# Moving a store and its reloads to another queue, weights ahead of parameters, three reorderings

## The reference

```python
def first_block(x, ...):                   # one layer
    h = rms_norm(x, norm1_w)
    z = h @ w_in                           # s5 mixer, differential attention, two gates
    m = sigmoid(gs) * (s5_mixer(z) @ w_proj_ssm) + sigmoid(ga) * (diff_attention(z) @ w_proj_attn)
    x = x + m @ w_out
    h = rms_norm(x, norm2_w)
    return x + (silu(h @ w_ffn_gate) * (h @ w_ffn_up)) @ w_ffn_down

def second_block(x, positions, ...):       # two layers
    for l in range(2):
        cb, cc, ch, cg, cq, ckv, kpe, mg, rcols, rg = split(x @ w_in[l])
        y_conv = cb * conv3(cc * ch) * silu(cg)
        q = (rms_norm(cq) @ w_uq)          # per head: 128 plain columns and 64 rotary ones
        kv = (rms_norm(ckv) @ w_ukv)
        y_mla = attention(q with rope(q_pe), k with rope(kpe), v) * silu(mg)
        y_rwkv = rwkv7(rcols) * silu(rg)
        x = layer_norm(4 ** 0.25 * x + concat(y_conv, y_mla, y_rwkv) @ w_out[l]) * ln_g + ln_b
    return x
```

## Time and profile before

| | us |
|---|---|
| median of three runs | 2587.32 |
| lowest, highest | 2584.78, 2589.74 |
| the profiled execution, its own time | 2588.43 |
| its span on the core | 2586.6 |
| mean granted TensorE clock, share of full | 0.985 |
| PE busy | 2484.6 (96% of the span) |
| DVE, ACT, POOL busy | 1475.0, 1130.2, 167.7 |

### The profile page before, as it was taken

How to read it: one execution, slowest core, us unless ns; L and a number is a source line. 1 busy time by engine, 2 the same in 40 slices (tenths; PEclk the granted TensorE clock), 3 DMA queues, 4 the chain that set the end, 5 groups by cost and what they waited for, 6 DMA issues and landing times.

```text
span 2586.6 us, 45207 instructions
## 1 busy us (share of the span) xinstructions
PE 2484.6 (96%) x19625; PEld 2259.6 (87%) x19625; DVE 1475.0 (57%) x1814; ACT 1130.2 (44%) x1562; POOL 167.7 (6%) x172
## 2 busy tenths in 40 slices
PE   6999999999989999999999999999999889999997
PEld 6777888999889999999888899999888789999885
DVE  3899955665445444454444446646555547455555
ACT  4565555544444444444333335324443525334442
POOL 4000000001000000000000002200000231200000
PEclk9999999999999999999999999999999889999998
DMA  7444444455546565655555565434537454235364
GB/s 206 136 155 139 155 142 129 131 188 174 188 140 183 180 185 182 184 183 182 187 186 187 182 202 158 119 88 122 148 127 240 135 181 141 88 102 163 104 198 161
DMA packets 261174, 412.43 MB, mean 159 GB/s; under 512 B 52912, under 2 KB 73776, under 8 KB 260464
## 3 DMA queue, kind: packets, MB, share of 16 engines
q1 hardware_dynamic: 259520, 408.22, 51.4%
q0 software_dynamic: 1424, 1.31, 0.3%
q10 hardware_dynamic: 32, 0.01, 0.0%
HBM read 403.17 MB, written 6.30 MB: 158 GB/s over the span
## 4 chain that ended last, share of the span: by engine, by line
PE 86%; DVE 7%; ACT 2%; SPq 2%; POOL 1%; issue 1%; DMA 1%; ACTq 0%; DVEq 0%
PE bank L569 85%; DVE wp_lo L1077 2%; ACT wp_hi L1727 1%; DMA raw<-w_in 1%; POOL xt L2305 1%; SPq L521 1%; SPq L510 1%; POOL xt L2303 0%; PE bank L776 0%; ACT L1727 0%; DVE r_a L1555 0%; DVE rsd L1202 0%; DVE nsd L1469 0%; DVE r_kb L1557 0%; DVE xr L1720 0%
## 5 line engine op out<-in xcount | busy, mean ns | idle before, releaser
L1077 DVE TENSOR_TENSOR wp_lo<-raw,wp_hi 128x1024 fp32r<-128x1024 f32 x740 | 919.5, 1249 | 950.9 <-ACT wp_hi L1727 949.7
L1727 ACT ACTIVATE wp_hi<-raw 128x1024 fp32r<-128x1024 f32 x740 | 783.4, 1061 | 1180.5 <-PE bank L569 1121.8
L569 PE MATMUL bank<-XX_hi,wp_hi 128*128 128x256 f32 x3840 | 1117.5, 291 | 42.4 <-DVE wp_lo L1077 26.0
L569 PE MATMUL bank<-XX_lo,wp_hi 128*128 128x256 f32 x3840 | 1091.4, 284 | 0.0
L569 PE MATMUL bank<-XX_hi,wp_lo 128*128 128x256 f32 x3840 | 1091.0, 284 | 0.0
L569 PEld LDWEIGHTS bank<-XX_hi,wp_hi 128*128 128x128 f32 x3840 | 741.4, 193 | 62.1 <-issue 37.8
L569 PEld LDWEIGHTS bank<-XX_lo,wp_hi 128*128 128x128 f32 x3840 | 741.9, 193 | 2.2 <-issue 1.9
L569 PEld LDWEIGHTS bank<-XX_hi,wp_lo 128*128 128x128 f32 x3840 | 741.2, 193 | 0.0
L569 PE MATMUL bank<-wp_hi,FF_hi 128*128 128x512 f32 x352 | 139.3, 396 | 0.0
L569 PE MATMUL bank<-wp_lo,FF_hi 128*128 128x512 f32 x352 | 139.1, 395 | 0.0
L569 PE MATMUL bank<-wp_hi,FF_lo 128*128 128x512 f32 x352 | 139.1, 395 | 0.0
(11 more groups left out here) (469 smaller groups left out, 2741.8 us busy)
## 6 DMA issues: line engine op xcount, KB each, us to landing
raw<-w_in SPq DMA_DIRECT2D x304, 512.0 KB, 3.8
raw<-w_out SPq DMA_DIRECT2D x96, 512.0 KB, 4.5
raw<-w_ffn_gate SPq DMA_DIRECT2D x88, 512.0 KB, 3.6
raw<-w_ffn_up SPq DMA_DIRECT2D x88, 512.0 KB, 3.7
raw<-w_ffn_down SPq DMA_DIRECT2D x88, 512.0 KB, 3.6
raw<-w_proj_attn SPq DMA_DIRECT2D x16, 512.0 KB, 4.2
raw<-w_proj_ssm SPq DMA_DIRECT2D x16, 512.0 KB, 3.6
raw<-w_glu SPq DMA_DIRECT2D x8, 512.0 KB, 3.3
```

The costliest lines, as they stand in the source:

```text
L569: return e.matmul(o, lhsT, rhs, start=start, stop=stop, skip_group_check=True)
L1077: return tt(d, src, hi, SUB)
L1727: return e.activation(o, x, func, bias=bias, scale=scale)
```

## The change

1. **The start.** Piece 3 is loaded ahead of the s5 parameters. `ssm_c` is loaded ahead of piece 6, positions and the second constants ahead of piece 8. A semaphore of its own (`s_c5`) covers `ssm_c`. In the first norm, ACT and DVE split each of the first three weight pieces ahead of the group of x instead of behind it.
2. **The norms at `wo3` and `xo3` of layer 0.** DVE evacuates the last job's banks first and splits the piece afterwards. ACT loads the table for the square root one job earlier.
3. **x for the residual.** POOL stores `kept`, for layer 0 once `fd3` is evacuated, for layer 1 behind its own last addition. POOL also reloads the quarters of `xr`, `lng` and `lnb`: the first behind the attention output, each other one when the job before it is over. DVE waits for each quarter by a semaphore of its own.
4. **The rotary part.** `pq` comes ahead of `nq0`. The rotary work on PE, POOL and DVE stands behind `nq0` instead of behind `kn1`, and `MXr_lo` behind `vn1`.

```diff
+        add(f"pq{l}", Wq, [(192 * i + 128, 64) for i in range(8)], 4, "AV")
         for c in range(2):
             add(f"nq{c}{l}", Wq, [(192 * (4 * c + i), 128) for i in range(4)], 4, "AV")
-        add(f"pq{l}", Wq, [(192 * i + 128, 64) for i in range(8)], 4, "AV")
...
-        for p in range(3):
+        for p in range(4):
             weights(p)
...
-        for p in range(3, NP):
-            for l, (name, s, value) in enumerate((("misc0", *freed("fd3", 1)), ("rk1", *YT("b", 7)))):
-                if p == OF[name].over:
-                    e.wait_ge(s, value)
-                    e.dma_start(tokens(kept[l]), xt).then_inc(s_kept, 16)
...
-                        e.dma_start(xr[:, :, w], tokens(kept[l])[:, :, w]).then_inc(s_xr, 16)
...
+        for p in range(4, NP):
+            if p == 6:
+                for d, name in ((X1, "ssm_c_re"), (X2, "ssm_c_im")):
+                    for q in range(2):
+                        e.dma_start(d[:, :, 64 * q:64 * q + 64], cv(name)).then_inc(s_c5, 16)
+            elif p == 8:
+                e.dma_start(posi[:, :], A["positions_2"][0].partition_broadcast(128)).then_inc(s_pos, 16)
+                e.dma_start(cst[:, NFIRST:NCONST], A["consts"][:, NFIRST:NCONST]).then_inc(s_cst, 16)
@@ tensor @@
-            main(at.until(f"kn1{l}"))
+            main(at.until(f"nq0{l}"))
             emptied(e, f"pq{l}")
@@ vector @@
-                e.wait_ge(s_xr, 16 * (4 * l + c + 1))
+                e.wait_ge(s_xr[c], 16 * (l + 1))
...
-                    if p + 3 < NP:
+                    if p + 3 < NP and not (t + 1 == ENDS[j.name] and j.name in ("wo3", "xo30")):
                         split(p + 3)
...
         for g in range(10):
+            if g < 3:
+                split(g)
             if g < 8:
                 rest_of_x(0, g)
-            if g < 3:
-                split(g)
...
         at.limit("fd3")
+        split(OF["wo3"].over + 2)
         roots(1)
...
-            main(at.until(f"kn1{l}"))
-            for i in range(2):
-                e.wait_ge(*RXA("h", 2 * l + i))
-                lo(MXr.lo(512 * i, 512 * i + 512), pair(mixT, 6 + i), ...)
+            main(at.until(f"nq0{l}"))
...
             main(at.until(f"vn1{l}"))
+            for i in range(2):
+                e.wait_ge(*RXA("h", 2 * l + i))
+                lo(MXr.lo(512 * i, 512 * i + 512), pair(mixT, 6 + i), ...)
...
+                    if g == 1:
+                        split(OF["xo30"].over + 2)
@@ scalar @@
+        main(at.until("wo2"))
+        e.preload_act_table(ACT.Sqrt)
         main(at.until("wo3"))
...
+            main(at.until(f"xo2{l}"))
+            e.preload_act_table(ACT.Sqrt)
             main(at.until(f"xo3{l}"))
@@ gpsimd @@
         main(at.until("fd3"))
+        e.wait_ge(*freed("fd3", 1))
+        e.dma_start(tokens(kept[0]), xt).then_inc(s_kept, 16)
...
             main(at.until(f"cb{l}"))
+            e.wait_ge(s_kept, 16 * (l + 1))
+            e.wait_ge(*MXV("l", 4 * l + 3))
+            for c in range(4):
+                w = slice(512 * c, 512 * c + 512)
+                if c:
+                    e.wait_ge(*over(f"xo{c - 1}{l}"))
+                e.dma_start(xr[:, :, w], tokens(kept[l])[:, :, w]).then_inc(s_xr[c], 16)
+                e.dma_start(lng[:, w], A["ln_g_2"][l, w].partition_broadcast(128)).then_inc(s_gb, 16)
+                e.dma_start(lnb[:, w], A["ln_b_2"][l, w].partition_broadcast(128)).then_inc(s_gb, 16)
...
+                e.wait_ge(*YT("b", 7))
+                e.dma_start(tokens(kept[1]), xt).then_inc(s_kept, 16)
```

More of the change, by code:

```diff
@@ L408, in program @@
                                              sem("s_out"))
-    s_kept, s_xr, s_gb = sem("s_kept"), sem("s_xr"), sem("s_gb")
+    s_c5 = sem("s_c5")
+    s_kept, s_gb, s_xr = sem("s_kept"), sem("s_gb"), [sem(f"s_xr{c}") for c in range(4)]
     s_hi, s_lo, s_mm = sem("s_hi"), sem("s_lo"), sem("s_mm")
@@ L522, in _ @@
         cv = lambda n: A[n][0].rearrange("g c p -> (g c) p").rearrange("(i q) p -> q i p", q=128)
[L523 to L529, removed]
-        for p in range(3, NP):
-            for l, (name, s, value) in enumerate((("misc0", *freed("fd3", 1)), ("rk1", *YT("b", 7)))):
-                if p == OF[name].over:
-                    e.wait_ge(s, value)
-                    e.dma_start(tokens(kept[l]), xt).then_inc(s_kept, 16)
[L535 to L541, removed]
-                        e.dma_start(xr[:, :, w], tokens(kept[l])[:, :, w]).then_inc(s_xr, 16)
-                    elif p == first_of(f"xo{c}{l}") + 6:
-                        e.dma_start(lng[:, w], A["ln_g_2"][l, w].partition_broadcast(128)).then_inc(s_gb, 16)
-                        e.dma_start(lnb[:, w], A["ln_b_2"][l, w].partition_broadcast(128)).then_inc(s_gb, 16)
+        for p in range(4, NP):
[6 more added lines that the diff above has]
+                e.dma_start(cst[:, NFIRST:NCONST], A["consts"][:, NFIRST:NCONST]).then_inc(s_cst, 16)
             for l, name in enumerate(("fd3", "xo30")):
@@ L588, in operand @@
                 e.wait_ge(*NL("l", 16 + 8 * int(l) + k // 2))
-            elif n == "nq0" and k % 2 == 0:
+            elif n == "pq" and k % 2 == 0:
                 e.wait_ge(*normed(f"cq{l}", k // 2))
@@ L696, in _ @@
         bank(5, *SV("li"))
-        e.wait_ge(s_s5, 16 * 11)
+        e.wait_ge(s_s5, 16 * 7)
         e.transpose(B[5][:, 0:32], lam[0][0:32, :], ident[0:32, 0:32])
@@ L1641, in _ @@
             at.limit(f"cb{l}")
-            main(at.until(f"kn1{l}"))
-            for i in range(2):
-                e.wait_ge(*RXA("h", 2 * l + i))
-                lo(MXr.lo(512 * i, 512 * i + 512), pair(mixT, 6 + i), MXr.hi_f(512 * i, 512 * i + 512)).then_inc(RXV.made("l", 2 * l + i), 1)
+            main(at.until(f"nq0{l}"))
             e.wait_ge(*ROA("cos"))
@@ L1658, in _ @@
             main(at.until(f"vn1{l}"))
+            for i in range(2):
+                e.wait_ge(*RXA("h", 2 * l + i))
+                lo(MXr.lo(512 * i, 512 * i + 512), pair(mixT, 6 + i), MXr.hi_f(512 * i, 512 * i + 512)).then_inc(RXV.made("l", 2 * l + i), 1)
             main(at.share(2))
@@ L2182, in _ @@
         at.limit("gs2")
-        e.wait_ge(s_s5, 16 * 11)
+        e.wait_ge(s_c5, 16 * 4)
         for q in range(2):
@@ L2216, in _ @@
         main(at.until("fd3"))
+        tokens = lambda a: a.rearrange("t p c -> p t c")
+        e.wait_ge(*freed("fd3", 1))
+        e.dma_start(tokens(kept[0]), xt).then_inc(s_kept, 16)
         def r_stage(l, c, i):
```

## The result

| | before | after |
|---|---|---|
| median, us | 2586.05 | 2548.69 |
| lowest, highest | 2583.93, 2589.74 | 2548.06, 2549.30 |
| span of the profiled execution | 2586.6 | 2546.4 |
| mean granted clock | 0.985 | 0.993 |

The ratio is 0.9854, 95% interval 0.9837 to 0.9871: 37.4 us saved, where 40.0 were forecast. The forecast of 2547 is 1.7 us low.

A forecast was written before the change was run, and what follows sets the result against it. PE, busy 96% of the span, was taken as the bound, so only its stops and slow clock could be won. Terms summing to 40.0 us, off 2588.4, left 2548.4; less 1.1 for the median, 2547 us, range 2538 to 2560.

The forecast's parts named there:

- The bound: Whole kernel: PE is busy 96% of the span, so only its standing still or running slowly can be won.
- The start: Opening loads: piece 3 asked for ahead of `sb` ends PE's 6.04 us wait; gain 6.0 + 1.5 = 7.5 us.
- The norms: Behind `wo3` and layer 0's `xo3`: banks emptied before the split, earlier table load; gains 2.9 and 2.3 us.
- The rotary part: Both layers: rotary work behind `nq0` ends PE's 4.57 us wait for `vM`; gains 6.7 and 5.6 us.
- The second store: Layer 1's x, stored from POOL's queue: PE's 12.5 us wait goes, plus 2.5 of clock; gain 15.0 us.
- The slack of 8.3 us: Second store: left of a weight piece's 14.4 us after landing, rounding and splitting; covers a neighbour's 5.8.
- The first store: Layer 0's x, stored by POOL amid `misc0`: taken as 0, between 2.2 us lost and 6.4 gained.
- One step of the weighing: First store: a DMA share of 0.79 just behind the store was cited for taking the term as 0.
- The reloads: `xr`, `lng` and `lnb` reloaded by POOL instead of SP: hidden, gain 0.
- the slower rival: POOL's reloads come too late in `xo1` to `xo3`: 2614 us, or 2599 by the skill's factor; chance 0.04.
- The sum: Whole kernel: 7.5 + 2.9 + 2.3 + 6.7 + 5.6 + 15.0 + 0 = 40.0 us saved.

The follow-up runs named there:

- e5: Changed kernel with the start's loads back in the old order, early splits kept: 2554.84 us, ratio 0.9888.
- e6: Changed kernel with only piece 3 ahead of `sb`; `X`, `posi` and `cst` stay ahead of piece 4: 2552.70 us, ratio 0.9877.
- e9: Changed kernel with the last piece's split ahead of the emptying of the banks again at `wo3` and layer 0's `xo3`: 2554.24 us, ratio 0.9876.
- e10: Changed kernel without the two early loads of the square root's table: 2551.74 us, ratio 0.9867.
- e7: Changed kernel with rotary work and `MXr_lo` back ahead of `vn0`, `pq` still first: 2560.15 us, ratio 0.9902.
- e8: Changed kernel with the six rotary operations back ahead of `vn0`, `MXr_lo` left behind `vn1`: 2552.94 us, ratio 0.9875.
- e3: Changed kernel with layer 1's store of x back on SP's queue: 2563.66 us, ratio 0.9909.
- e2: Changed kernel with layer 0's store of x back on SP's queue behind `misc0`: 2547.53 us, ratio 0.9845.
- e1: Changed kernel with POOL's store of x for layer 0 held until the last piece of `misc0` is split: 2541.50 us, ratio 0.9824.
- e4: Changed kernel with the reloads of `xr`, `lng` and `lnb` back on SP's queue: 2548.85 us, ratio 0.9851.
- e12: Kernel of e11 plus 15 more unused products while PE waits ahead of the s5 weights: 2540.29 us, ratio 0.9819.
- e11: Kernel of e1 plus 16 unused identity products during PE's waits behind `wo3` and layer 0's `xo3`: 2539.40 us, ratio 0.9819.

## Why the prediction was right

**The bound.** Right: PE's stops were the time. DVE and ACT are as busy as before.

**The start**: 7.5 forecast, 7.8 by the traces, 6.1 by e5. Piece 4 is covered only because `X` moved behind piece 5 (e6). The splits ahead of x's groups were put at nothing; the traces leave them half a microsecond at most (e5).

**The norms**: 2.9 at `wo3` was the order (1.7) and the table load (1.2). Measured one by one, the waits give 2.0 (e9) and 1.1 (e10); their sum 3.1 is what PE's wait lost (6.85 to 3.77). The stretch in the table above gained 3.3. The half clock there also fell, from 6.9 to 3.3 us, and brought no more than the other 0.2. At `xo3` 2.3, the order alone, as forecast.

**The rotary part**: 12.3 forecast, 11.5 by e7. Both waits fell away whole. The 0.3 us that short jobs' evacuation should still cost is there (0.32 at 1836.83), but in each layer PE also stops for 0.70 us that the sum left out (1830.63 in layer 0). It is the start of `kn1`, which needs the banks of `nq1`: DVE's second copy of `qn` ends at 1830.53, because it stands behind the six rotary operations and two splits. So the 4.1 us of rotary work are not hidden whole, though the prediction took them to be. The stop is absent in e7 and e8. `pq` first cost nothing that shows, as it said.

**The second store**: 15.0 forecast, 15.0 by e3. The slack of 8.3 us covers a neighbour: no PE wait over 0.6 us beside it. The 17.4 of the traces holds half clock behind `xo3` that is not the store's: the kernel before has 13.6 us of it, 5.7 of them inside this stretch with PE busy throughout, half of which is lost (2.8); the changed kernel has 3.4, all ahead of it.

**The first store** was the unclear term, 0 within -2.2 to 6.4, with a PE wait of 3 to 6 us inside `misc0`. The wait is there, 4.85 us. The term is -1.4 by the two traces and -1.2 by e2's median, neither clear of noise: in the nine kernels that store x there as the changed one does (itself, e3 to e10), this stretch takes 755.6 to 757.4 us, in the kernel before 756.0, in e2 754.3. So the range holds the term, and its sign is likely, not shown. The Trainium skill ("DMA: Bandwidth & Descriptors", Queues, rings and completion order) says that a DMA engine empties a whole packet of one queue before it turns to the next; from this the prediction had worked out a delay near the full 5.8 us. The fifth piece of `misc0` is 5.4 us later than in e1, so the delay came out that way; the packets themselves no run shows. One step of the weighing was wrong: a DMA share of 0.79 was read as room, but that window lies behind the store. Beside it the kernel before has 0.94 (1508 to 1516), and beside its own store, where the piece came late, the changed kernel has 1.01:

```profile
1487.00:1495.00 8.00, 7.91 (x66) 7.56 (x64) 1.23 (x1) 1.06 (x1) 0.04 (x1) 1.00 1.01 348
```

(A row of the changed kernel.) What the prediction didn't ask is whether the store could come later: nothing waits for it before the scan. e1 does that and saves 7.2 us more, ratio 0.9824.

**The reloads**: nothing, as forecast (e4). `xr` lands in 5.8 us from POOL's queue, 5.3 from SP's, a store in 9.6 against 7.9. The factor of five between 620 and 3100 ns, which the Trainium skill states ("SBUF — State Buffer", SBUF: two separate sides) for a DMA from GpSimd's queue beside a DVE copy, doesn't show in these larger transfers beside a DVE that mostly splits weights, and the slower rival did not come.

**The sum** came out 2.6 us high against the medians. Against the spans it looks exact, 40.0 for 40.2, and that is in part luck: the second store's stretch gained 2.4 more than its term, through the clock, and the stretch of the first store and those of the rotary part and `xo3` gained 1.4 less each (13.2 for 14.6). That the medians give 37.4 and not 40.2 lies mostly in the starting point: the profiled execution of the kernel before, from which the forecast was taken, was 2.4 us slower than its median of four.

## What to carry to other kernels

A large transfer that nothing waits for soon is placed by the slack of its neighbours, not by when its data are ready. Put it on a queue whose engine has nothing to feed, if the store has to wait for its data: SP's wait of 15.0 us held up the weights behind it (e3). And hold it back until the tight transfers have landed: POOL's queue at the early place left a stop of 4.85 us, SP's behind `misc0` one of 2.97, POOL's with three pieces of `rk0` asked for ahead of it none (e1, e2). And a stop of PE costs more than its length, so work out the stop from rows, and keep two or three microseconds open for the clock.

## What the runs showed of the hardware that I had not expected

The stretches at half clock differ where the code doesn't. The stop near 362 us is 1.73 us long in every one of these kernels, and behind it the clock stays up in the changed one and falls in e2, e6 and e12 (the row of the changed kernel first, then that of e6):

```profile
364.00:372.00 8.00, 8.00 (x45) 5.88 (x45) 4.51 (x14) 4.30 (x11) 0.00 (x0) 1.00 0.10 36
```

```profile
364.00:372.00 8.00, 8.00 (x28) 5.82 (x28) 1.95 (x9) 4.72 (x10) 0.00 (x0) 0.62 0.23 68
```

From there to 512 us PE needs 3.0 us more in e2 and e6 than in the changed kernel. Behind `xo3`, with 4.53 us of waiting in all of them, the half clock lasted 3.4 us in the changed kernel, e4 and e6, 6.9 in e1, 10.2 in e2, e3, e5, e7, e8 and e10. So up to 3 or 4 us of a profile's difference between two kernels can come from none of their edits. Waits of PE that end with an engine's work repeat to 0.1 us in all kernels that have the same code there (3.76 to 3.77 behind `wo3`, 4.53 behind `xo3`, 4.57 for `vM`) and are the better witness. Waits that end with a load don't: the one inside `misc0` is 4.53 to 5.20 us in nine kernels with the same store, and the one at the start 6.04 before and 5.00 in e5. Products without use kept the clock up through a stop of 3.7 to 4.5 us in both places of e11 and in two of three of e12.

A split by DVE takes 1.23 us alone and 2.2 us beside POOL's multiplications (1820.42 above, where POOL multiplies from 1820.27 to 1823.77; seen in the traces, not tested alone). And two transfers side by side moved 390 GB/s at a DMA share of 1.01 (e1), so full engines don't by themselves say that PE will wait.
